# Last two experts' outputs kept on chip and added by weighted one-hot products

## The reference, cut to what matters

```
scores = sigmoid(x @ w_router); best group, then the top 2 experts in it
w = w / w.sum(-1)                                  # weights of the two
for e in range(16):
    h = silu(x @ wg[e]) * (x @ wu[e])
    y = y + combine[:, e:e+1] * (h @ wd[e])
x <- LN(ALPHA * x + y)
```

## Time and profile before

| | us |
|---|---|
| median of 3 runs | 1206.39 |
| lowest and highest | 1197.67, 1210.31 |
| the profiled execution's own time | 1204.36 |
| its span, first to last instruction | 1202.8 |
| PE busy | 1060.8 (88%) |
| DVE busy | 890.2 (74%) |
| ACT busy | 710.1 (59%) |
| POOL busy | 207.6 (17%) |
| mean granted TensorE clock | 0.941 |

### The profile page before, as it was taken

One profiled execution on the slowest core, in us unless ns is written; L12 is line 12 of the kernel. 1 busy time (PEld: TensorE's weight loads), 2 busy tenths in 40 slices (PEclk: granted clock), 3 DMA queues, 4 the chain that ended last, 5 costly groups with the idle time before them and its releaser, 6 DMA issues.

```text
span 1202.8 us, 16880 instructions
## 1 busy us (share of the span) xinstructions
PE 1060.8 (88%) x5460; PEld 888.5 (74%) x5460; DVE 890.2 (74%) x1136; ACT 710.1 (59%) x871; POOL 207.6 (17%) x182
## 2 busy tenths in 40 slices
PE   5999799989989999999289987999799999999950
PEld 4987598877878888887178866888677888888840
DVE  2683865378979988887747737735899798888947
ACT  2423665265768887877433246723577787787852
POOL 3000000014632111210220000100173311222120
PEclk9999889998999999999589988999899999999985
DMA  9523111217999999997824212002499999999934
GB/s 301 160 77 105 51 38 44 88 72 275 356 358 380 388 382 377 381 379 278 251 72 166 61 62 88 27 18 105 134 308 360 378 389 383 379 383 384 378 122 151
DMA packets 117061, 273.26 MB, mean 227 GB/s; under 512 B 10305, under 2 KB 13345, under 8 KB 116993
## 3 DMA queue, kind: packets, MB, share of 16 engines
q1 hardware_dynamic: 98608, 227.36, 52.1%
q0 software_dynamic: 17088, 42.45, 10.6%
q10 hardware_dynamic: 1296, 2.62, 0.7%
HBM read 262.02 MB, written 25.22 MB: 239 GB/s over the span
## 4 chain that ended last, share of the span: by engine, by line
PE 52%; DMA 20%; DVE 10%; issue 6%; ACT 5%; POOL 3%; DVEq 2%; ACTq 0%; SPq 0%; POOLq 0%
DMA raw_far<-in_w_gate 14%; PE bankA L1666 9%; PE bankB L1666 7%; PE bankA L1915 7%; PE bankB L1915 5%; PE bankC L1666 4%; PE bankD L1666 4%; PE bankC L1938 3%; PE bankD L1938 3%; POOL slot_rows L673 3%; DVE w_lo L427 3%; PE bankG L1739 2%; ACT w_hi L421 2%; PE bankE L1655 2%; PE bankF L1655 1%
## 5 line engine op out<-in xcount | busy, mean ns | idle before, releaser
L427 DVE TENSOR_TENSOR w_lo<-raw,w_hi 128x2048 fp32r<-128x2048 f32 (+1 forms) x152 | 340.8, 2262 | 55.5 <-ACT w_hi L421 51.4
L421 ACT ACTIVATE w_hi<-raw 128x2048 fp32r<-128x2048 f32 (+1 forms) x152 | 287.4, 1896 | 138.7 <-PE bankC L1666 46.1
L427 DVE TENSOR_TENSOR w_lo<-raw_far,w_hi 128x2048 fp32r<-128x2048 f32 x64 | 146.4, 2288 | 15.3 <-ACT w_hi L421 15.3
L421 ACT ACTIVATE w_hi<-raw_far 128x2048 fp32r<-128x2048 f32 x64 | 122.8, 1919 | 50.3 <-PE bankB L1915 22.0
L1915 PE MATMUL bankA<-w_hi,xe_hi 128*128 128x512 f32 x256 | 101.8, 398 | 3.8 <-DVE xe_lo L442 3.6
L1915 PE MATMUL bankB<-w_hi,xe_hi 128*128 128x512 f32 x256 | 102.6, 401 | 1.3 <-DVE w_lo L427 1.3
L1915 PE MATMUL bankA<-w_lo,xe_hi 128*128 128x512 f32 x256 | 100.6, 393 | 0.0
L1915 PE MATMUL bankA<-w_hi,xe_lo 128*128 128x512 f32 x256 | 100.6, 393 | 0.0
L1915 PE MATMUL bankB<-w_hi,xe_lo 128*128 128x512 f32 x256 | 100.1, 391 | 0.0
L1915 PE MATMUL bankB<-w_lo,xe_hi 128*128 128x512 f32 x256 | 99.9, 390 | 0.0
L653 POOL DMA_INDIRECT y_rows<-expert_out,idx x32 | 53.2, 1662 | 173.4 <-ACT expert_out L928 171.0
(11 more groups left out here) (373 smaller groups left out, 2539.6 us busy)
## 6 DMA issues: line engine op xcount, KB each, us to landing
raw<-in_w_up SPq DMA_DIRECT2D x64, 1024.0 KB, 7.3
raw_far<-in_w_gate SPq DMA_DIRECT2D x60, 1024.0 KB
raw<-in_w_down SPq DMA_DIRECT2D x60, 1024.0 KB, 12.4
raw<-in_w_in SPq DMA_DIRECT2D x12, 1024.0 KB, 6.5
raw<-in_w_o SPq DMA_DIRECT2D x8, 1024.0 KB, 6.2
x_rows<-x POOLq DMA_DIRECT2D x10, 512.0 KB, 3.0
raw<-in_w_gate SPq DMA_DIRECT2D x4, 1024.0 KB
raw_far<-in_w_down SPq DMA_DIRECT2D x4, 1024.0 KB
```

The source lines that it names most:

```text
L421: act.activation(w_hi[:, s % RB, :, 0:n], raw_unit(s)[:, :, 0:n], ACT.Copy).then_inc(hi_done, 1)
L427: dve.tensor_tensor(w_lo[:, s % RB, :, 0:n], raw_unit(s)[:, :, 0:n], w_hi[:, s % RB, :, 0:n].bitcast(F32), ALU.subtract).then_inc(lo_done, 1)
```

## The change

Experts 0 to 13 are handled as before. The outputs of experts 14 and 15 are no longer scattered to DRAM: they stay in `expert_out`, and are added to the rows of x by matrix products. For each of the two experts and each tile of rows, a 128x128 matrix `own` has the row's weight where the row's rank in the expert equals the column, and zero elsewhere. POOL makes these ten matrices, PE transposes them, ACT copies them to `own_t`, and PE multiplies each by `expert_out`, two experts accumulated in one bank of 512 columns, two halves to a tile (`own_sum`). DVE adds the banks to x (`add_own`). Since rows that no expert 0 to 13 sends would be stale, y2_dram is first filled with the kernel's input rows, and the weights of outputs that don't come from it are set to zero (`pick1`, `pick2`). SP instead of POOL loads both outputs from y2_dram, the second ones first, into `y_second` (where `xe_hi` and `xe_lo` are) and `y_first`. PE makes own_sum 0 to 2 ahead of the next layer's head, in layer 0 own_sum(3) after tile 0's projection and own_sum(4) ahead of tile 1's, in layer 1 both directly. ALPHA\*x moves ahead of the last expert's copy on ACT. The first four weight units of a layer are issued before SP's loop (layer 0) and at the end of its body (layer 1).

The diff, cut to its core:

```diff
+    for name, bank in ((("own", 0), "E"), (("own", 1), "F"), (("own", 2), "H")):
+        fill(name, bank)
+    for t in range(NT):
+        for h in range(2):
+            fill(("sum", t, h), ("AB", "CD", "GH", "GH", "GH")[t][h])
...
+        y_second = over(base_t, "y_second", [P, NT - 1, D], at=24576) 
+        own = over(base_m, "own", [P, 2, NT, P], at=18432)
+        own_t = over(base_m, "own_t", [P, 2, 4 * P], at=26624)
...
         @block.sync
+            for s in range(RB):
+                load_proj(0, s)
             with sp.Fori(0, DEPTH) as l:
...
                 overflow(sp, l, past, block_units, held_sp, units_used)
+                with sp.If(l < DEPTH - 1):
+                    for s in range(RB):
+                        load_proj(l + 1, s, DEPTH - 1)
+                for c in range(2):
+                    sp.wait_ge(out_free[c], (NE // 2) * (l + 1))
+                wait_filled(sp, "up", l, 0, NE - 1)
+                load_outputs(1)
+                sp.wait_ge(lo_done, RX + UNITS * (l + 1))
+                load_outputs(0)
...
         @block.gpsimd
                 pool.dma_start(gmv_sample[l, 0], gv[0:DEC, 4, :]).then_inc(kv_out, 16)
+                for j in range(2):
+                    for r0, n, src in ((0, SEQ, x_prompt[0]), (SEQ, DEC, x_sample[0])):
+                        pool.dma_start(y2_dram[2 * r0:2 * (r0 + n), :].rearrange("(p j) n -> p j n", j=2)[:, j, :], src) \
+                            .then_inc(y2_filled, 16)
...
-                for e in range(NE - 1):
+                hold(y2_filled, 64 * (l + 1))
+                for e in range(NE - 2):
                     if e + 4 < NE:
                         gather_next(e + 4)
                     send(e)
-                def outputs_early():
-                    hold(lo_done, RX + UNITS * (l + 1))
-                    load_outputs(0, range(2))
-                    send(NE - 1, lambda: load_outputs(0, range(2, NT)))
+                hold(own_w_done, l + 1)
+                for e in range(2):
+                    for t in range(NT):
+                        ins = pool.tensor_scalar(own[:, e, t, :], own_iota[:, :], own_rank[:, t, e:e + 1], own_w[:, t, e:e + 1],
+                                                 ALU.is_equal, ALU.mult)
+                ins.then_inc(own_done, 1)
...
         @block.scalar
                 hidden_hi(0, NE - 1)
+                act.wait_ge(x1_out, 16 * NT * (l + 1))
+                for t in range(NT):
+                    act.activation(x[:, t, :], x[:, t, :], ACT.Copy, scale=ALPHA).then_inc(scaled, 1)
+                def own_out():
+                    for e in range(2):
+                        wait_filled(act, ("own", e), l)
+                        read(act.activation(own_t[:, e, :], bank_of(("own", e))[:, :], ACT.Copy), ("own", e))
+                    wait_filled(act, ("own", 2), l)
+                    read(act.activation(own_t_last[:, :, :], bank_of(("own", 2))[:, 0:2 * P].rearrange("p (e n) -> p e n", e=2),
+                                        ACT.Copy), ("own", 2))
+                def last_out():
+                    expert_rows_out(0, NE - 1)
+                    own_out()
...
                     with act.If(l < DEPTH - 1):
                         for s in range(2):
                             next_split(s)
-                    expert_rows_out(0, NE - 1)
+                    last_out()
...
         @block.vector
                 round_of(0, NE - 1, SO_LAST)
-                hidden_lo(0, NE - 1)
                 picked(s1, score[:, :], pick1)
                 picked(s2, score[:, :], pick2)
...
                 dve.reciprocal(srec, ssum)
+                hidden_lo(0, NE - 1)
+                dve.tensor_scalar(own_in[:, :, :], own_rank[:, :, :], float(P) - far, None, ALU.is_lt)
+                dve.tensor_tensor(own_w[:, :, :], tiles(score[:, :], NT)[:, :, NE - 2:], own_in[:, :, :], ALU.mult)
+                dve.tensor_tensor(own_w[:, :, :], own_w[:, :, :], srec.unsqueeze(2).to_broadcast([P, NT, 2]), ALU.mult)
+                dve.sem_inc(own_w_done, 1)
+                dve.tensor_scalar(own_in[:, :, :], own_in[:, :, :], -1.0, 1.0, ALU.mult, ALU.add)
+                for v in (pick1, pick2):
+                    mine = tiles(v[:, :], NT)[:, :, NE - 2:]
+                    dve.tensor_tensor(mine, mine, own_in[:, :, :], ALU.mult)
+                picked(s1, score[:, :], pick1)
+                picked(s2, score[:, :], pick2)
...
-                def add_first(t):
+                def add_sent(t):
                     dve.wait_ge(scaled, NT * l + t + 1)
+                    dve.wait_ge(y_second_in[t], 16 * l + 16)
+                    add_output(t, 1, y_second[:, t, :] if t < 4 else y_second_last[:, :])
                     dve.wait_ge(y_first_in[t], 16 * l + 16)
+                    dve.drain()
                     add_output(t, 0, y_first[:, t, :] if t < 4 else y_first_last[:, :])
-                def add_second(t):
+                def add_own(t):
+                    for h in range(2):
+                        part = x[0:n, t, h * HALF:(h + 1) * HALF]
+                        wait_filled(dve, ("sum", t, h), l)
+                        read(dve.scalar_tensor_tensor(out=part, in0=bank_of(("sum", t, h))[0:n, :], scalar=1.0, in1=part,
+                                                      op0=ALU.mult, op1=ALU.add, accum_out=mv[0:n, t, h:h + 1]), ("sum", t, h))
+                    dve.drain()
+                    dve.tensor_scalar(mv[:, t, 0:1], mv[:, t, 0:1], mv[:, t, 1:2], -1.0 / D, ALU.add, ALU.mult).then_inc(mean_done, 1)
...
         @block.tensor
                 down(SO_LAST + 6, 0, NE - 1)
+                pe.wait_ge(own_done, l + 1)
+                for e in range(2):
+                    turn(("own", e), l, [own[:, e, t, :] for t in range(4)])
+                turn(("own", 2), l, [own[:, e, 4, :] for e in range(2)])
+                def own_sum(t):
+                    for h in range(2):
+                        wait_free(pe, ("sum", t, h), l)
+                        for e in range(2):
+                            mine = own_t[:, e, t * P:(t + 1) * P] if t < 4 else own_t_last[:, e, :]
+                            ins = pe.matmul(bank_of(("sum", t, h))[:, :], mine, expert_out[:, e, h * HALF:(h + 1) * HALF],
+                                            start=(e == 0), stop=(e == 1))
+                        done(ins, ("sum", t, h))
-                overflow(pe, l, past, block_pe, held_pe)
+                overflow(pe, l, past, block_pe, held_pe, blocks_sent, own_read)
+                for t in range(3):
+                    own_sum(t)
                 with pe.If(l < DEPTH - 1):
-                    head(l + 1)
+                    head(l + 1, own_sum)
+                with pe.If(l > DEPTH - 2):
+                    for t in range(3, NT):
+                        own_sum(t)
```

More of the change, by code:

```diff
@@ L258, in build @@
         r5 = [over(base_m, f"r5_{k}", [P, NT], at=3 * QB + 3840 + 32 * k) for k in range(7)]
+        own_rank, own_in, own_w = (over(base_m, f"own_{k}", [P, NT, 2], at=3 * QB + 4064 + 64 * k) for k in range(3))
         local = over(base_m, "local", [P, 2 * NT], at=2 * QB + 8 * D)
@@ L686, in gather_next, with send @@
                     gather(e, idx[:, e, 1:2])
-                def send(e, beside=None):
+                def send(e):
                     for c in range(2):
@@ L1007, in no_blocks @@
                     act.sem_inc(held_act, 1)
[L1009 to L1013 removed]
+                overflow(act, l, past, block_act, held_act, after_blocks, last_out, no_blocks)
                 act.activation(warm[:, 0:1], eps, ACT.Sqrt)
@@ L1691, in turn_rows, with head @@
                     turn(("xt", t, h), l, [x[:, t, (4 * h + k) * P:(4 * h + k + 1) * P] for k in range(4)])
-            def head(l):
+            def head(l, own_sum=None):
                 turn_rows(l, 0)
                 for t in range(NT):
+                    if t == 1 and own_sum is not None:
+                        own_sum(NT - 1)
                     if 2 <= t + 1 < NT:
@@ L1701, in head @@
                     if t == 0:
+                        if own_sum is not None:
+                            own_sum(NT - 2)
                         turn_rows(l, 1)
```

103 lines of the change are left out of this document (66 added, 37 removed).

## The result

The changed kernel takes 1222.14 us in the median of four runs (1221.29 to 1228.30), the kernel before 1208.35 in the same comparison: a ratio of 1.014, 95% interval 1.0105 to 1.0175. It is slower by 13.8 us between the medians and by some 17 us by the ratio; 1210 was predicted, with 1221 as the upper end. The profiled execution took 1221.64 us.

A forecast was written before the change was run, and what follows sets the result against it. Bound by PE's products and weight loads, with each layer's first closing addition on DVE deciding the ends; +6.0 in layer 0 and -2.2 in layer 1 give +3.8 on the median 1206.39: 1210 us, range 1202 to 1221.

The forecast's parts named there:

- GpSimd's one-hots: Ten 128x128 matrices on POOL after own_w in each layer: 0.45 us each, done at 570.5 and 1160.5, hidden.
- The points from which they count: Price per matrix beyond which each us delays the layer once: 0.67 us in layer 0, about 0.80 in layer 1.
- GpSimd at its row: Rival: matrices take 1.06 us each, 3.9 in layer 0 and 2.6 in layer 1, +4.8 in all: 1215; chance 0.25.
- the ends of the two rows: POOL's TENSOR_SCALAR (1.02, 1.10 us) ended 0.48 or 0.49 behind the start of DVE's second L1187 instruction in both layers.
- DVE's branch in layer 1: Ahead of layer 1's ten additions on DVE: loading count_max and the branch take 1.6 us together.
- the sum's -4.6: Layer 1's first closing addition on DVE starts at 1172.8 instead of 1177.44, 4.6 us earlier.
- layer 1's -2.2: Layer 1 in total: -4.6 for the first closing addition, +0.7 for five tiles, +1.7 waiting for sum 3.
- The rest of layer 0: Layer 0's first closing addition 4.3 us later; PE leaves the next layer's head 6.0 us late.
- The wait for sum 3: Layer 1: own sum 3 runs at PE's lower clock, so DVE waits about 1.7 us for its second half.
- Costed at nothing: Filling y2_dram, two scatters fewer a layer and SP's loads ahead of its loop: all taken as 0 us.
- The fill: Filling y2_dram (4.7 MB) lies under projections, 0 us; rival: it delays the mask load, +8 us, 1218, chance 0.06.
- one rival: GpSimd's matrices dearer than forecast: some of this rival sets the range's upper end, 1221.

The follow-up runs named there:

- tail_order: Changed kernel with DVE's branch for layer 1's tail placed ahead of the one for layer 0's tail; 1223.05 us, ratio 1.017 to the kernel before.
- both edits: Changed kernel with the ten matrices made by DVE instead of GpSimd, and layer 1's tail ahead of layer 0's in DVE's code; 1212.27 us, ratio 1.0041.
- early_own: Against the kernel with both edits: rows' weights computed ahead of the expert loop, matrices ahead of the last h_lo; 1215.80 us, ratio 1.0064.
- reordered: early_own, plus ACT splitting two weight units before scaling x and DVE's w_lo moved into layer 0's tail; 1213.19 us, ratio 1.0064.
- mid_weights: reordered, but with y2_dram filled in layer 0 alone and the rows' weights computed in iteration 3 of the expert loop; 1210.85 us, ratio 1.0045.

## Why the prediction was wrong, step by step

The order of what waits for what was right, and the failure lies in two terms of the sum: the price of GpSimd's matrices was put at 0.45 us instead of 0.78 and more, and the stand at DVE's branch in layer 1 was not in it at all.

- **GpSimd's one-hots** ("I take 0.45 each, nearer to CAST ... hidden"). They took 1.16 each in layer 0 and 0.78 in layer 1. The points from which they count were right in layer 0: (1.16 - 0.67) x 10 = 4.9 us in layer 0 against 9.1 - 4.3 = 4.8 measured, and 0.78 is just under the 0.80 of layer 1, where nothing came of it while DVE stood at its branch (without the stand, in tail_order, they took 1.38 each). This is the rival "GpSimd at its row", its 3.9 in the first layer and none in the second. I had read the ends of the two rows as a wait for DVE. That may be so, though both end 0.5 us inside DVE's second instruction, which a full exclusion would not allow; but even with a wait of 0.2 or 0.3 there stands a price of 0.78 that CAST does not show. And I took DVE to be on few columns while the matrices are made: two w_lo of 128x2048 fell in, and one matrix waited for both, 4.6 us. The Trainium skill's rule on two SBUF inputs (SBUF — State Buffer, Who interferes with whom), named in the prediction, is borne out by these (4.6 beside 4.49; 13.76 us beside the additions against 7.80). The prediction's estimate of 0.2 us a matrix, from the 1.8 cycles an element of the Trainium skill (GPSIMD Engine Reference, 3.1 Elementwise — side-by-side cycle accounting), is not.
- **DVE's branch in layer 1** ("the load of count_max and the branch take 1.6 (the 1.62 in the earlier trace rows)"). That row is layer 0's, where nothing is skipped; in layer 1 DVE jumps over the whole tail of layer 0, which had grown from 96 records to 121. That the growth made the difference is not shown. The stand there was 4.97 us, the sum's -4.6 became +0.4, and layer 1's -2.2 became +2.2 by the first profiles. With the early loads moved away it was 2.4, on one profile. No rival named it.
- **The rest of layer 0** was right: the kernel with both faults mended has the first closing addition 27.2 us after h_hi, 3.8 over the mean of the two profiles of before (4.3 forecast), and the third projection 61.1, 6.0 over (6.0 forecast). That the second agrees so well is luck in part: 0.5 us less up to the closing addition and 0.5 more behind it cancel, and this date moves by 1.3 us between profiles. Own sums, ten additions, the clock of the second projection were sized rightly.
- **The rest of layer 1**: with both edits the first closing addition comes 1.8 us earlier; -4.6 plus 2.5 for the matrices on DVE is -2.1. The wait for sum 3 was 1.56 (1.7). In layer 1 the early loads kept up (at most 0.2 us of waiting) wherever DVE starts its additions 6 us or more after h_hi; in early_own, reordered and mid_weights, where it starts after 2.3 to 2.7, it waits 3.1 to 3.9 us for a first output.
- **Costed at nothing.** The fill, rightly. What the prediction left out is how far the middle of the kernel moves by chance: between the ends the two profiles of the changed kernel took 541.1 us in the mean, the two of before 536.5. Of the 17 us, layer 0's end is 11.2 (66.3 against 55.1), layer 1's 2.8 (46.6 against 43.8), and some 3 are left. Since kernels without the change range from 533.4 to 538.0 and kernels with it from 531.5 to 542.1, I can't say that the change put them there, nor that it didn't.
- **The range.** It reached to 1221 by part of one rival. Each of the two faults alone gives 1215 (1206.4 + 3.8 + 4.9 or + 5.0), both 1220, at the very edge, and the few us of chance or of the comparison's higher median (1208.35) did the rest. Faults add, and the chances treated the rivals as exclusive.

## What to carry to other kernels

An engine's price for an operation is read from that operation or bounded by its own row, not by the friendlier neighbour, and a wait that the row shows comes on top of the price rather than in place of it. A taken branch can cost a load of code, here 2.4 to 5.1 us where the trace shows one and 0.1 to 0.5 where it doesn't: put first the body that is not to wait, and look at what stands between the branch and its target in each pass of a loop. Two causes that end at the same date hide each other, so an experiment on one alone may show nothing; judge by the dates inside the layer and not by the whole time, which moves by 1% with nothing changed.

## What the hardware showed that I had not expected

- At a taken branch over the other layer's tail DVE stood 4.97 to 5.07 us in four profiles and 2.4 in a fifth, with the DMA engines at 3 GB/s. Over a body of one and the same length (the other tail) it stood 2.8 and 3.3 us in reordered and mid_weights and 0.5 in tail_order and early_own. In the two long ones the DMA engines moved 264 and 272 GB/s, in the two short ones nothing and 80, and the branch stood elsewhere in the code; which of the two decides is not shown.
- GpSimd's TENSOR_SCALAR with two per-row operands on 128x128 fp32 takes 0.78 us, DVE's 0.34, ten in 2.7.
- Issuing an indirect DMA on GpSimd takes 1.0 to 1.1 us where none of DVE's instructions with two inputs in SBUF runs at its start (55 issues in three profiles), and up to 3.1, mostly 1.6 or more, where one does. At expert 4's gather that is a wait of some 3 us for PE that comes and goes.
